# Scan levels: odd heads on the other half of the partitions, the transposed inverse by TensorE and ScalarE, inner keys behind the levels

## The reference, cut to what matters

```
def rwkv_scan(S0, r, w, k, v, a, b, reverse):
    def step(S, inp):
        r_t, w_t, k_t, v_t, a_t, b_t = inp
        sa = jnp.einsum('bhij,bhj->bhi', S, a_t)
        S = S * w_t[:, :, None, :] + sa[..., :, None] * b_t[:, :, None, :] + v_t[..., :, None] * k_t[:, :, None, :]
        return S, jnp.einsum('bhij,bhj->bhi', S, r_t)
```

## Time and profile before

| | |
|---|---|
| median of 3 runs | 2395.57 us |
| profiled execution | 2394.62 us |
| its span in the trace | 2392.8 us |
| TensorE busy | 2200.9 us (92%) |
| VectorE busy | 998.3 us (42%) |
| ScalarE busy | 675.8 us (28%) |
| GpSimd busy | 772.4 us (32%) |
| the three visits of the first layer | 529 to 666 us |
| the three visits of the second layer | 1797 to 1930 us |
| levels of the second visit, first layer | 584.9 to 605.8 us |

### The profile page before, as it was taken

How to read it: one execution, slowest core, us unless ns; L and a number is a source line. 1 busy time by engine, 2 the same in 40 slices (tenths; PEclk the granted TensorE clock), 3 DMA queues, 4 the chain that set the end, 5 groups by cost and what they waited for, 6 DMA issues and landing times.

```text
span 2392.8 us, 45856 instructions
## 1 busy us (share of the span) xinstructions
PE 2200.9 (92%) x19352; PEld 1772.0 (74%) x19352; DVE 998.3 (42%) x1512; ACT 675.8 (28%) x1184; POOL 772.4 (32%) x546
## 2 busy tenths in 40 slices
PE   5999988889989899999999889988888988999997
PEld 3888566559966688888888668846658965888886
DVE  3002355476653732414142420336566646442443
ACT  3110355742222211112111221045552223221221
POOL 2333333014131223232222343235205133444443
PEclk9999999989999899999999989999999989999998
DMA  6221100120022211111123231110030023232231
GB/s 260 80 69 54 71 1 0 57 72 4 4 80 69 82 62 62 61 61 62 61 68 129 92 111 55 45 71 0 0 129 3 5 80 123 93 97 91 96 96 61
DMA packets 45412, 162.55 MB, mean 68 GB/s; under 512 B 5504, under 2 KB 5504, under 8 KB 45024
## 3 DMA queue, kind: packets, MB, share of 16 engines
q1 hardware_dynamic: 44480, 157.89, 19.4%
q0 software_dynamic: 800, 2.69, 0.3%
HBM read 158.46 MB, written 2.10 MB: 67 GB/s over the span
## 4 chain that ended last, share of the span: by engine, by line
PE 79%; DVE 13%; ACT 4%; issue 3%; DMA 1%; SPq 0%; POOL 0%; ACTq 0%; POOLq 0%; DVEq 0%
PE ps L1462 76%; DVE small L1162 2%; PE ps L1777 2%; DVE part_h L1060 1%; DVE hT L1053 1%; ACT flat L775 1%; DVE xT L1078 1%; DVE flat L1446 1%; ACT flat L793 1%; DVE ps L1159 1%; DVE flat L1076 1%; DMA flat<-wmod_dram 1%; PE ps L2038 0%; DVE part_h L1331 0%; DVE flat L1341 0%
## 5 line engine op out<-in xcount | busy, mean ns | idle before, releaser
L1462 PE MATMUL ps<-part_hi,wparts 128*128 128x512 f32 (+1 forms) x3072 | 827.2, 356 | 27.6 <-DVE part_h L1060 9.5
L1462 PEld LDWEIGHTS ps<-part_hi,wparts 128*128 128x128 f32 x3072 | 548.1, 191 | 122.4 <-DVE part_h L1060 15.4
L526 POOL TENSOR_TENSOR wparts<-flat,wparts 128x1024 fp32r<-128x1024 f32 x184 | 446.4, 2426 | 534.5 <-ACT wparts L975 528.8
L1462 PE MATMUL ps<-part_h,wparts 128*128 128x512 f32 (+1 forms) x1536 | 545.3, 355 | 0.0
L1462 PE MATMUL ps<-flat 64*64 64x32 f32 (+8 forms) x8812 | 474.4, 259 | 54.1 <-ACT flat L793 28.6
L1462 PEld LDWEIGHTS ps<-flat 64*64 64x64 f32 (+4 forms) x8812 | 364.7, 141 | 154.0 <-issue 75.4
L1462 PE MATMUL ps<-part_mlp,wparts 128*128 128x512 f32 (+1 forms) x1536 | 417.1, 358 | 14.6 <-DVE part_h L1060 9.7
L1462 PEld LDWEIGHTS ps<-part_h,wparts 128*128 128x128 f32 x1536 | 296.2, 193 | 38.9 <-issue 1.7
L1462 PEld LDWEIGHTS ps<-part_mlp,wparts 128*128 128x128 f32 x1536 | 275.1, 191 | 62.1 <-DVE part_h L1060 11.7
L975 ACT ACTIVATE wparts<-flat 128x1024 fp32r<-128x1024 f32 x112 | 118.8, 1061 | 703.7 <-PE ps L1462 703.7
L1462 PE MATMUL ps<-part_lo,wparts 128*128 128x512 f32 (+1 forms) x768 | 272.0, 354 | 0.0
(11 more groups left out here) (202 smaller groups left out, 1938.3 us busy)
## 6 DMA issues: line engine op xcount, KB each, us to landing
flat<-w_dram SPq DMA_DIRECT2D x128, 512.0 KB, 3.4
flat<-wmod_dram SPq DMA_DIRECT2D x88, 512.0 KB, 5.6
flat<-win_dram SPq DMA_DIRECT2D x40, 512.0 KB, 3.5
flat<-wout_dram SPq DMA_DIRECT2D x16, 512.0 KB, 3.6
hT<-wmod_dram SPq DMA_DIRECT2D x8, 512.0 KB, 8.7
xT<-xT_dram SPq DMA_DIRECT2D x8, 384.0 KB, 6.7
flat<-rope_dram SPq DMA_DIRECT2D x2, 1024.0 KB, 5.5
out_dram<-xT SPq DMA_DIRECT2D x8, 256.0 KB, 2.0
```

Of the source, the lines that this page charges most:

```text
L526: pool.tensor_tensor(wlo[q % 2], src, whi[q % 2], ALU.subtract).then_inc(s_used[q], 1)
L1462: return pe.matmul(out, lhsT, rhs, start=start, stop=stop)
```

## The change

1. The first product X writes the odd heads (p = 1) to the other half of the partitions and to another bank, in the order `FOUR`; the second product T reads them there and writes back to its own half. VectorE's mask covers the same 256 columns in two banks. Its add is split in two, one for the even and one for the odd heads (128 columns each).
2. TT is no longer made by VectorE. Ahead of each X group TensorE multiplies TN with the identity (16 matmuls of 64 columns, `s_tr`), and ScalarE copies the result from PSUM to TT (128x512, `s_tt`). This is done at all five levels; before, four levels had a transpose, since the first TT came from the start of the visit.
3. `seen` moves from level 1 to behind Z, half by half; ScalarE's copies of it (AV) follow those of Z.
4. At the first level the first group now waits for `s_ane` and `s_ke` (ScalarE's copies of the inputs a and of the keys), whose banks it overwrites; ScalarE makes them half by half. The bonus matmuls stand behind T of level 2. ScalarE's copies for the output projection (`out_part`) in the third visit are spread over the levels.
5. Two semaphores are merged or dropped (`s_maskraw`, `s_seen`), with no other effect on the order.

```
 # VectorE
-  V.tensor_tensor(cells(-1, HALF[x] + XM, [128, 2], [32, 4], [1, 32]),
-                  bank(-1, 2048 * x, [128, 2], [32, 4], [1, 32]), ...
+  V.tensor_tensor(cells(-1, HALF[x] + XM, [128, 2], [64, 2], C1),
+                  bank(-1, 2048 * x, [512, 2], [64, 2], C1), ...
-  t = cells(-1, HALF[x] + TN, [256 + half, 2], [2 * half, 128 // half], [1, half])
-  V.tensor_tensor(t, t, bank(-1, 2048 * x + 1024, [128, 2], ...), ALU.add).then_inc(s_tn[x], 1)
-  if j < len(LEVELS) - 1:
-      dve.wait_ge(s_tn[x], 6 * n + j + 2)
-      V.transpose(cells(-1, HALF[x] + TT, [1, 512]), cells(-1, HALF[x] + TN, [1, 512])).then_inc(s_tt[x], 1)
+  for p in range(2):
+      t = cells(-1, HALF[x] + TN + p * P, [256 + half, 2], [2 * half, 64 // half], [1, half])
+      ins = V.tensor_tensor(t, t, bank(-1, 2048 * x + 1024 + p * 512, [64, 2], ...), ALU.add)
+  ins.then_inc(s_tn[x], 1)
 # ScalarE
+  def transposed(n, j):
+      for x in range(2):
+          act.wait_ge(s_tr[x], 5 * n + j + 1)
+          nc_.activation(cells(-1, HALF[x] + TT, [P, 2], [256, 2], [1, P]),
+                         bank(-1, 2048 * x + 1280, [512, 2], [P, 2], [1, P]), ACT.Copy).then_inc(s_tt[x], 1)
 # TensorE, each level
   pe.wait_ge(s_tn[x], 6 * n + j + 1)
+  if j == 0:
+      pe.wait_ge(s_ane[x], n + 1)
+      pe.wait_ge(s_ke[x], n + 1)
-  for g in range(2): for p in range(2): for f in range(2): for c in range(2):
-      ins = mm(bank(c, o + g * P + (2 * p + f) * 32, [1, 32]), ABR block, TN block [32 columns])
+  for g in range(2): for f in range(2): for p, c in FOUR:
+      ins = mm(bank(c ^ p, o + 1280 + p * 512 + g * P + f * 64, C1), TN block,
+               kf[64 * c:64 * c + 64, K_ID * P + 64 * c:K_ID * P + 64 * c + 64])
+  ins.then_inc(s_tr[x], 1)
+  for g in range(2): for f in range(2): for p, c in FOUR:
+      ins = mm(bank(c ^ p, o + p * 512 + f * 64 + g * 32, [1, 32]), ABR block, TN block [32 columns])
   ins.then_inc(s_X[x], 1)
...
   pe.wait_ge(s_Xm[x], 5 * n + j + 1)
-  pe.wait_ge(s_ke[x], n + 1) if j == 0 else pe.wait_ge(s_tt[x], 4 * n + j)
+  pe.wait_ge(s_tt[x], 5 * n + j + 1)
   (T group, now with FOUR; reads partitions of c ^ p, writes those of c)
-  if j == 1: seen(x)
 # TensorE, behind the levels
   (Z group of x)
   ins.then_inc(s_Z[x], 1)
+  seen(x)
```

More of the change, by code:

```diff
@@ L212, in backbone @@
         AS, ASPREAD = 2900, (2048, 3072, 2048, 3072, 2048)
-        KS, BONUS = 3844, 2048 + 1024 + 256
+        KS, BONUS = 3844, 2048 + 512 + 256
         kd, gtok = wv(W_KD, 4, TOK), wv(W_G, NB, 256)
@@ L288, in backbone @@
         s_pool = sem("s_pool")
-        s_atab = sem("s_atab")
+        s_tables = sem("s_tables")
         s_psq = sem("s_psq")
@@ L346, in backbone @@
         s_av, s_ave = pair("s_av"), pair("s_ave")
-        s_X, s_Xm, s_Tp = pair("s_X"), pair("s_Xm"), pair("s_Tp")
+        s_X, s_Xm, s_Tp, s_tr = pair("s_X"), pair("s_Xm"), pair("s_Tp"), pair("s_tr")
         s_Z, s_Za, s_Zd = pair("s_Z"), pair("s_Za"), pair("s_Zd")
@@ L910, in _ @@
                                        ACT.Copy).then_inc(s_ke[x], 1)
-                    for x in range(2):
                         act.wait_ge(s_an[x], n + 1)
@@ L914, in _ @@
                                        ACT.Copy).then_inc(s_ane[x], 1)
[L915 to L929, removed]
+                    for j in range(len(LEVELS)):
+                        transposed(n, j)
+                        if s == 0 and j == 0:
+                            act.wait_ge(s_bonin, 2 * (l + 1))
+                            for f in range(2):
+                                ins = nc_.activation(bonus_in[:, f, :], bonus_in[:, f, :], ACT.Identity,
+                                                     scale=par(l, "r_k", f))
+                            ins.then_inc(s_gate, 1)
+                        if s == 0 and j == 2:
+                            act.wait_ge(s_bonps, l + 1)
+                            nc_.activation(bon[:, :], ps[:, BONUS:BONUS + NB * 4], ACT.Copy).then_inc(s_bon, 1)
+                        if s == STEPS - 1 and j < 4:
+                            out_part(OUT_ORDER[j], t)
                     for x in range(2):
@@ L933, in _ @@
                                        ACT.Copy).then_inc(s_Za[x], 1)
+                        act.wait_ge(s_av[x], n + 1)
+                        nc_.activation(cells(-1, HALF[x] + AV, [1, 512]), ps[:, 2048 * x + 1536:2048 * x + 2048],
+                                       ACT.Copy).then_inc(s_ave[x], 1)
                     for x in range(2):
@@ L1108, in _ @@
                 if l == 0:
-                    dve.wait_ge(s_maskraw, 16)
+                    dve.wait_ge(s_tables, 16)
                     V.tensor_copy(km[:, :], zT[:, 0:NKM]).then_inc(s_masks, 1)
@@ L1125, in _ @@
                                                in1=r, op0=ALU.mult, op1=ALU.mult).then_inc(s_pn, 1)
-                dve.wait_ge(s_atab, 64 * (l + 1))
+                dve.wait_ge(s_tables, 16 + 64 * (l + 1))
                 for n, (where, tile) in enumerate(ROPES):
@@ L1350, in _ @@
                             dve.wait_ge(s_X[x], 5 * n + j + 1)
[L1351 to L1353 removed]
+                            V.tensor_tensor(cells(-1, HALF[x] + XM, [128, 2], [64, 2], C1),
+                                            bank(-1, 2048 * x, [512, 2], [64, 2], C1),
+                                            bass.AP(km, m, [[NKM, P], [0, 2], [0, 2], C1]),
                                             ALU.mult).then_inc(s_Xm[x], 1)
@@ L1356, in _ @@
                             dve.wait_ge(s_Tp[x], 5 * n + j + 1)
-                            t = cells(-1, HALF[x] + TN, [256 + half, 2], [2 * half, 128 // half], [1, half])
-                            V.tensor_tensor(t, t, bank(-1, 2048 * x + 1024, [128, 2], [half, 128 // half], [1, half]),
-                                            ALU.add).then_inc(s_tn[x], 1)
-                            if j < len(LEVELS) - 1:
-                                dve.wait_ge(s_tn[x], 6 * n + j + 2)
-                                V.transpose(cells(-1, HALF[x] + TT, [1, 512]),
-                                            cells(-1, HALF[x] + TN, [1, 512])).then_inc(s_tt[x], 1)
+                            for p in range(2):
+                                t = cells(-1, HALF[x] + TN + p * P, [256 + half, 2], [2 * half, 64 // half], [1, half])
+                                ins = V.tensor_tensor(t, t, bank(-1, 2048 * x + 1024 + p * 512, [64, 2],
+                                                                 [half, 64 // half], [1, half]), ALU.add)
+                            ins.then_inc(s_tn[x], 1)
                     for x in range(2):
@@ L1952, in _ @@
                             pe.wait_ge(s_tn[x], 6 * n + j + 1)
-                            for g in range(2):
[L1954 to L1960, removed]
@@ L1961, in _ @@
-                            ins.then_inc(s_X[x], 1)
+                            if j == 0:
+                                pe.wait_ge(s_ane[x], n + 1)
+                                pe.wait_ge(s_ke[x], n + 1)
+                            if s == 0 and j == 3 and x == 1:
+                                pe.wait_ge(s_bon, l + 1)
+                            for g in range(2):
+                                for f in range(2):
+                                    for p, c in FOUR:
+                                        ins = mm(bank(c ^ p, o + 1280 + p * 512 + g * P + f * 64, C1),
+                                                 cells(c, h + TN + g * 256 + (2 * p + f) * 64, C1),
+                                                 kf[64 * c:64 * c + 64, K_ID * P + 64 * c:K_ID * P + 64 * c + 64])
@@ new lines, in _ @@
+                            ins.then_inc(s_tr[x], 1)
+                            for g in range(2):
+                                for f in range(2):
+                                    for p, c in FOUR:
+                                        ins = mm(bank(c ^ p, o + p * 512 + f * 64 + g * 32, [1, 32]),
+                                                 cells(c, h + ABR + p * 512 + f * 256 + g * P, C1),
+                                                 cells(c, h + TN + g * (256 + half) + (2 * p + f) * 64,
+                                                       [2 * half, 32 // half], [1, half]))
@@ new lines, in _ @@
+                            ins.then_inc(s_X[x], 1)
+                        for x in range(2):
+                            h, o = HALF[x], 2048 * x + 1024
+                            pe.wait_ge(s_Xm[x], 5 * n + j + 1)
+                            pe.wait_ge(s_tt[x], 5 * n + j + 1)
+                            for g in range(2):
+                                for f in range(2):
+                                    for p, c in FOUR:
+                                        ins = mm(bank(c, o + p * 512 + g * 64 + f * 32, [1, 32]),
+                                                 cells(c ^ p, h + TT + g * 256 + (2 * p + f) * 64, C1),
```

(2 more changed lines are left out.)

6 lines of the change are left out of this document (2 added, 4 removed).

## The result

The kernel after takes 2449.32 us, the median of four runs (2443.78 to 2452.06); before, run beside it, 2396.86 us. The ratio is 1.0224, 95% interval 1.0208 to 1.0240: slower by 52 us. The forecast was 2434 us, slower, within 2408 to 2464.

The account below looks back on a forecast made before the run. TensorE was taken to bound the levels before, arriving instruction blocks those after. Levels 26.2 + `seen` 1.9 - 20.9 = +7.2 us a visit; six visits +43, two bonus stretches -4: +39 us, 2434 us, range 2408 to 2464.

Parts of the forecast that it names:

- The bound of before, and the pace: Levels before: bound by TensorE at 29.3 ns a record on two quadrants; four quadrants would run at 14.5 ns.
- The chain of 3.15 us a level: Levels after: TensorE groups, VectorE's adds and waits would take 3.15 us a level instead of 3.75, if blocks cost nothing.
- Blocks of 128 records: TensorE's instructions arrive in blocks of 128 records; a level of 192 records is 1.5 blocks, 5.5 us, and stops.
- room for two blocks: Instruction fetch: room for the block in use and one more; the next is asked for when one is used up.
- The time of a block: Levels after: each instruction block needs at least 3.65 us, with 3.3 and 4.0 as bounds.
- The prediction's bounds: Block time at its limits: 3.3 us gives +4.8 a visit, 2420 us; 4.0 us gives +9.5, 2448 us.
- `seen` at its old price behind the levels: Behind or between the Z groups: its 64 records at 29.3 ns cost 1.9 us a visit, as inside the levels.
- The clock: Rival, chance 0.10: stops lower the granted clock too; half clock in Z and `seen` adds 32 us, 2466 us.
- The rest: Outside the scan: nothing of weight is moved, so 0 us for all but the levels and Z.
- Rival A: Levels: instruction blocks stay hidden, a level takes 3.15 us, and the kernel gets faster, 2379 us; chance 0.11.
- C: Levels: four quadrants bring nothing at 32 columns, 5.6 us a level without stops, 2449 us; chance 0.06.
- the narrower range: Whole kernel: the forecast's own range if blocks bind, 2416 to 2450 us, chance 0.70.

Follow-up runs that it names:

- the bench: Not a changed kernel: TensorE alone runs five lists of 384 matmuls (768 records) with 64x64 weights, wide matmuls between them; the lists took 12.4 to 22.6 us.
- filler: Kernel after with two matmuls of 384 columns (4 records) added behind the T groups of every level, result unread: 2453.75 us, 1.0243 of before.
- full_tr: Kernel after with the 16 identity matmuls of each half and level replaced by 4 transposes of 128x128, VectorE's add in four pieces: 2399.04 us, 1.0014 of before.
- the loop of 24 rounds: The four-quadrant, 32-column list of 384 matmuls, run as 24 rounds of 16 instead of written out: 15.0 us, against 20.0 us written out.
- double_tr: Kernel after with the 16 identity matmuls of each half and level issued twice in a row: 2502.44 us, 1.0445 of before.
- list e: TensorE alone, 384 matmuls on four quadrants with 64 columns, written out: 768 records in 19.9 us.
- list d: TensorE alone, 384 matmuls on two quadrants with 32 columns, written out: 22.6 us, without a stop.
- list a: TensorE alone, 384 matmuls on four quadrants with 32 columns, written out: 20.0 us, part of it at a granted clock of 0.50.
- late_mix: Kernel before with `seen` behind the levels and TensorE's order there seen 0, Z 0, seen 1, RM 0, Z 1, N 0, RM 1, N 1: 2395.94 us, 1.0003.

## Why the prediction was right, and what it had too small

*The bound of before, and the pace.* Right. Inside a group the levels after run at 14.5 ns a record at full clock, and the lists of the bench give the same paces without a scan around them. The chain of 3.15 us a level can't be read whole, since the blocks bind in its place; its parts fit.

*Blocks of 128 records.* Right, and the term that decides. Four kernels with 136, 192, 196 and 256 records a level order by records, not by work: filler adds 36 us of work inside the levels and they grow by 1.3, full_tr has the work of after and 2.5 us of its loss of 52. That instructions come from a transfer queue in blocks of 16 KB is seen in the DMA rows; that the stop is a wait for them is shown by the loop of 24 rounds, which has neither, and by the restarts, which come 1.2 to 1.6 us after the end of a transfer in all 82 intervals. That there is room for two blocks fits (the next transfer begins only after a restart, with the queue idle before it), but no run varied it.

*The time of a block.* The term that was too small. 3.65 us was taken; the 30 pairs of stops (over 0.15 us) 127 or 128 records apart in the kernel after have a mean of 3.79 us (3.45 to 4.46), the 42 of double_tr the same 3.79. 45 blocks (7.5 x 6) times 0.14 us are 6.3 us. The levels of the kernel after took 166.4 us where the prediction's terms give 159.8 (6 x 26.2 and two bonus stretches of 1.3): 6.6 us over. The other 1.2 of the 7.8 us are in before: 20.9 us was read from the slowest visit without a bonus, the other three took 20.6. The prediction's bounds are also slightly off as sums: 3.3 us a block gives +4.6 a visit (it has +4.8) and 4.0 gives +9.8 (it has +9.5), 2418 and 2449 us in all; it changes nothing.

*`seen` at its old price behind the levels.* Right where the clock stood: 5.30 us from Z to RM, 5.4 predicted.

*The clock.* Given a chance of 0.10 as a rival in which it falls everywhere. It came in part and beside the forecast: the granted clock was 0.50 for 61 us in the two stretches 538 to 702 and 1832 to 2003 (in before it was 1.00 through all levels of both layers, and from Z to RM). TensorE had been busy 5.72 of the 8.20 us ahead of the fall at 663.2 (70%); in the levels of the sixth visit it was busy 17.02 of 26.10 us (65%) and the clock stayed at 1.00. In the levels, where the blocks bind, it cost little: six intervals between restarts with a lower clock have a mean of 3.96 us, the 23 at full clock 3.74. It cost 1.4 to 1.7 us in each of three Z stretches (6.97, 6.71 and 6.95 us against 5.30), 4.7 us in all. The Z stretch of the sixth visit took 5.67 us at a granted clock of 1.00: there TensorE paused 0.3 us inside `seen`, 128 records behind the last restart. The window of the slow Z of the second visit, and of the fast one of the fifth:

```profile
622.80:629.40 6.60, 6.60 (x132) 6.60 (x127) 1.72 (x4) 1.74 (x3) 0.00 (x0) 0.79 0.03 5
```

```profile
1914.50:1919.70 5.20, 5.20 (x122) 5.20 (x124) 1.63 (x4) 1.71 (x3) 0.00 (x0) 1.00 0.03 6
```

*The rest.* All that lies outside the levels and Z: 3.2 us, against 0; no run shows what it is. (The new waits of the first level and the bonus matmuls are in the row of the levels.) In sum 38.8 were predicted; 7.8 for the levels, 5.0 for Z and 3.2 make it 54.8, by which the spans differ. The miss is 13 us of 52, and 2449 lies at the edge of the narrower range, 2416 to 2450.

*Rival A*, blocks hidden, fell with the stops inside the levels; *C*, four quadrants without a gain, by the pace between the stops and list e. The time alone could not have told C from the forecast: C had 2449 us.

The Trainium skill (Runtime: NRT & Kernel Launch, "Instruction fetch mechanics") has the block of 256 instructions right: 128 records of two instructions. Its "mostly hidden" holds in the bench for list d, 29 ns a record, and fails for list e, 14.5 ns: there 6 blocks cost 8.8 us beside 11.1 us of work. Its warning about taken branches is for a target outside the blocks at hand, which no run here has; the loops of the bench are 64 and 192 instructions long, and for them the page's preference for full unrolling did not hold: written out the list takes 20.0 us, looped 12.4.

## What to carry to other kernels

Count instructions as well as columns: straight-line TensorE code got about 128 records (a 32-bit matmul is two) each 3.6 to 3.8 us here, so a change that makes small matmuls denser gains only until a record costs some 29 ns, and one that adds matmuls beyond that pays 28 to 29 ns for each record however cheap it is. The sign of it in a profile is "issue" as releaser in the middle of a group, at equal counts of records, with a transfer of the instruction queue that ended a little over a microsecond before each restart. The remedies that worked here are fewer, larger instructions for the same work (4 transposes for 16 matmuls gave back 50 us) and, in the bench alone, a short loop.

## What was not expected of the hardware

- Half clock removes the stops: in list a of the bench, records of 29 ns at 0.50 ran through without one, so for such code a lower clock costs little (in after 61 us of it cost 4.7 us in Z and, as an estimate from the six intervals, about 1.3 us in the levels).
- The time of a block is not constant: 3.45 to 3.73 us in the bench, up to 4.46 us in the scan. The part from the end of the transfer to the restart hardly varies (1.20 to 1.47 us in after); what varies is when the transfer begins (1.05 to 2.04 us after a restart) and how long it takes (0.88 to 1.67). What sets these two stays open.
- A stretch of slow matmuls ahead of fast ones did not keep the stops away (Z, at 55 ns a record, ends at 609.2 in before, and TensorE stops ahead of 614.78), but spreading them (late_mix) did not pay either, though the stops became 2.8 us shorter in all.
